# Attention in a hybrid decoder block: score and value products as three fp32r products of parts

## Chip, cores, metric

The kernel runs on 1 core of one Trainium2 chip. The time is the device time of one execution in microseconds; a run's figure is that of its slowest core, here its only one. Engines are named as in the profile: PE is TensorE's matmul, PEld its weight load, DVE is VectorE, ACT is ScalarE, POOL is GpSimd, SP is SyncE.

## What is computed

One layer over 256 tokens of width 2048, all in float32. The part that the change touches is the attention branch: 16 heads of 128, causal, softmax with a linear bias. With one block of 256 tokens only the own block counts, so per head it is:

```python
q = rms_norm(q, q_norm_w);  k = rms_norm(k, k_norm_w)          # (256, 128) each
s = q @ k.T * 128 ** -0.5 - slope * (t_q - t_k)                 # masked where t_q < t_k
p = softmax(s)                                                  # (256, 256), lower triangle
attn = p @ v                                                    # (256, 128)
```

Around it stand the input projection (x @ w_in, 2048 x 18496), a Mamba-2 SSD branch, the output projections, gates, and an MLP of width 8192. Those weight products make nearly all of the work.

## The kernel before

**The weight stream.** All large products run as a stream of blocks. A block is 2048 rows by 512 columns of a weight matrix, taken in 8 units of 256 rows. SP loads a unit into one of four `raw` slots; ACT rounds it to fp32r (`whi`, L941); DVE subtracts to get the rest (`wlo`, L1463); PE runs 12 products of 512 columns per unit (L645 to L647: x_hi whi, x_hi wlo, x_lo whi). ACT and DVE work three units ahead of PE (`LEAD = 3`). On each engine the other work is put into this stream by hand: `steps(b, {step: [functions]})` on ACT and DVE runs the functions of a step behind the split of the unit three ahead; `stream(..., after={s: [...]})` on PE runs them behind unit s. Each engine runs its instructions in the order written.

**Attention.** The 16 heads go in four groups of four. Group g's q, k and v come out of the blocks 3g, 3g+1 and 3g+2. ACT copies them out of PSUM (L1009 to L1019), they are normed, turned by DMA transposes of their 16-bit halves and joined by DVE in `qk_both` (`q_join` L1575, `k_join` L1586). ACT copies `qk_both` with the norm weight to `qT` (L1037) and `kT` (L1053). The heads of group g run within the next three blocks (24 steps), five steps apart: scores on PE behind step 5h+1, bias and maximum on DVE, exp on ACT, the norm on DVE, the halves on ACT, a DMA transpose from SP's queue, `p_join` on DVE at step 5h+6 (L1631, L1633, out to `probT`), weights times values on PE behind step 5h+7, and the split of the result into `aT_hi` and `aT_lo` (L1077, L1639).

Causality leaves 3 of 4 tiles. So a head has one score product of 256 columns (queries of the second half against all keys, L718) and one of 128 (first half, L719), and in the same way one value product of 256 columns (L695) and one of 128 (L696). All four are plain fp32. PE shows a plain fp32 product as two records, an fp32r product as one.

**Other small products** of the kernel stay as they are: the dt projection in fp32r with 256 columns (L737 to L741), the SSD products in fp32 with 64 columns (L818), three fp32r products of 512 columns (L806), fp32 ones of 256 and 128 columns (L829, L830), and transposes of 128 columns (L597).

Of the kernel before, what the change touches and what calls it, by code (L numbers as in the profile page):

```python
# [23 lines left out]
T = 256  # L24
P = 128
NTOK = T // P
HD = 128
# [16 lines left out]
COLS = 512  # L44
# [8 lines left out]
B_QKV = 0  # L53
# [8 lines left out]
def build(nc, x, mix_norm_w, w_in, q_norm_w, k_norm_w, conv_w, conv_b, dt_bias, a_log, d_skip, ssm_norm_w,  # L62
          w_attn_out, w_ssm_out, w_out, mlp_norm_w, w_up, w_down, out):
    f32 = mybir.dt.float32
    f32r = mybir.dt.float32r
# [10 lines left out]
    with ctx:  # L76
# [6 lines left out]
        def sb(name, region, off, shape, dt=f32):  # L83
            return nc.alloc_sbuf_tensor_at(name, shape, dt, offset=BASE + at[region] + off)
# [16 lines left out]

        q_st = sb("q_st", "C", 0, [P, NTOK, COLS])
        k_st = sb("k_st", "C", 4 * KB, [P, NTOK, COLS])
        v_st = sb("v_st", "C", 8 * KB, [P, NTOK, COLS])
        sq = sb("sq", "C", 12 * KB, [P, 8, HD])
        qT = sb("qT", "C", 16 * KB, [P, 4, T])
        kT = sb("kT", "C", 20 * KB, [P, 4, T])
        qk_half = sb("qk_half", "E", 0, [P, 2, NTOK, COLS], u16)
        q_tiles = sb("q_tiles", "E", 4 * KB, [P, 2, NTOK * 4, P], u16)
        k_tiles = sb("k_tiles", "E", 12 * KB, [P, 2, NTOK * 4, P], u16)  # L110
        qk_both = sb("qk_both", "E", 8 * KB, [P, 4, T])
        prob = sb("prob", "C", 24 * KB, [P, 3 * P])
        probT = sb("probT", "C", 24 * KB + 1536, [P, 3 * P])
        dist = sb("dist", "C", 24 * KB + 3072, [P, 3 * P])
        dist_i = sb("dist_i", "C", 24 * KB + 4608, [P, 3 * P], i32)
        p_half = sb("p_half", "C", 24 * KB + 4608, [P, 2, 3 * P], u16)
# [112 lines left out]
        def sem(name):  # L229
            return ctx.enter_context(nc.semaphore(name))  # L230
# [64 lines left out]
        p_halved = sem("p_halved")  # L295
        p_turned = sem("p_turned")
        probT_ready = sem("probT_ready")
        pv = sem("pv")
        aT_hi_done = sem("aT_hi_done")
        aT_lo_done = sem("aT_lo_done")  # L300
# [74 lines left out]
        def fp(ap):  # L375

            return ap.bitcast(f32)

        def halves(ap):
            return ap.bitcast(u16).rearrange("p (n a) -> p a n", a=2)  # L380
# [212 lines left out]
        def _(pe):  # L593
# [94 lines left out]
            def at_pv(n, hh, g):  # L688
                def f():
                    pe.wait_ge(probT_ready, n + 1)  # L690
                    if hh == 0:
                        pe.wait_ge(set_free[2], g + 1)
                    if later(n):
                        pe.wait_ge(aT_lo_done, n)
                    mm(ps[7][:, 0:T], v_st[:, 0, hh * HD:(hh + 1) * HD], probT[:, 0:T], start=True, stop=False)  # L695
                    mm(ps[7][:, P:T], v_st[:, 1, hh * HD:(hh + 1) * HD], probT[:, T:T + P], start=False,  # L696
                       stop=True).then_inc(pv, 1)
                return f

            def attention(g):  # L700

                n0 = 4 * g
                a = [{} for _ in range(3)]

                def put(step, f):
                    a[step // 8].setdefault(step % 8, []).append(f)
                put(1, lambda: pe.wait_ge(kT_ready, g + 1))
                put(1, lambda: pe.wait_ge(qT_ready, g + 1))
                for hh in range(4):
                    put(5 * hh + 1, at_scores(n0 + hh, hh))  # L710
                    put(5 * hh + 7, at_pv(n0 + hh, hh, g))
                return a

            def at_scores(n, hh):
                def f():
                    if later(n):
                        pe.wait_ge(biased, n)
                    mm(ps[6][:, 0:T], qT[:, hh, P:T], kT[:, hh, :], start=True, stop=True)  # L718
                    mm(ps[6][:, T:T + P], qT[:, hh, 0:P], kT[:, hh, 0:P], start=True, stop=True).then_inc(scores, 1)  # L719
                return f  # L720

            def par_transposes():
# [208 lines left out]
        def _(act):  # L931
# [81 lines left out]
            def evac_v(g):  # L1013
                def f():
                    block_done(B_QKV + 3 * g + 2)
                    if later(g):
                        act.wait_ge(pv, 4 * g)
                    A(v_st[:, 0, :], SETS[2][0][:, :], ACT.Copy, scale=rstd1[:, 0:1])
                    A(v_st[:, 1, :], SETS[2][1][:, :], ACT.Copy, scale=rstd1[:, 1:2]).then_inc(set_free[2], 1)  # L1019
                return f  # L1020

            def q_halve(g):
# [8 lines left out]
            def copy_qT(g):  # L1031
                def f():
                    act.wait_ge(q_joined, g + 1)
                    act.wait_ge(const_ready, 2)
                    if later(g):
                        act.wait_ge(scores, 4 * g)
                    A(qT[:, :, :], qk_both[:, :, :], ACT.Copy, scale=par[:, QN_C:QN_C + 1]).then_inc(qT_ready, 1)  # L1037
                return f

            def k_halve(g):  # L1040
# [7 lines left out]
            def copy_kT(g):  # L1048
                def f():
                    act.wait_ge(k_joined, g + 1)  # L1050
                    if later(g):
                        act.wait_ge(scores, 4 * g)
                    A(kT[:, :, :], qk_both[:, :, :], ACT.Copy, scale=par[:, KN_C:KN_C + 1]).then_inc(kT_ready, 1)  # L1053
                return f

            def at_exp(n):
# [9 lines left out]
            def p_halve(n):  # L1066
                def f():
                    act.wait_ge(normed, 2 * n + 2)
                    if later(n):
                        act.wait_ge(p_turned, 16 * n)  # L1070
                    A(p_half[:, :, :], halves(prob[:, :]), ACT.Copy).then_inc(p_halved, 1)
                return f

            def at_hi(n):
                def f():
                    act.wait_ge(pv, n + 1)
                    A(aT_hi[:, bass.ds(n, 1), :].rearrange("p a t -> p (a t)"), ps[7][:, 0:T], ACT.Copy) \  # L1077
                        .then_inc(aT_hi_done, 1)
                return f

            def attention(n0):
                a = [{} for _ in range(3)]

                def put(step, f):
                    a[step // 8].setdefault(step % 8, []).append(f)
                for hh in range(4):
                    put(5 * hh + 3, p_halve(n0 + hh))
                for hh in range(4):
                    put(5 * hh + 2, at_exp(n0 + hh))
                    put(5 * hh + 8, at_hi(n0 + hh))  # L1090
                return a
# [363 lines left out]
        def _(dve):  # L1455
# [119 lines left out]
            def q_join(g):  # L1575
# [7 lines left out]
                    i.then_inc(q_joined, 1)  # L1583
                return f

            def k_join(g):  # L1586
                def f():
                    dve.wait_ge(k_turned, 32 * g + 32)
                    dve.wait_ge(qT_ready, g + 1)
                    for a in range(2):  # L1590
                        i = V.tensor_copy(halves(qk_both[:, :, :].rearrange("p c t -> p (c t)"))[:, a, :],
                                          k_tiles[:, a, :, :].rearrange("p (t c) l -> p c t l", t=NTOK))
                    i.then_inc(k_joined, 1)
                return f
# [31 lines left out]
            def p_join(n):  # L1626
                def f():
                    dve.wait_ge(p_turned, 16 * n + 16)
                    if later(n):
                        dve.wait_ge(pv, n)  # L1630
                    V.tensor_copy(halves(probT[:, :])[:, :, P:3 * P],  # L1631
                                  p_tiles[:, :, 0:2, :].rearrange("p a c l -> p a (c l)"))
                    V.tensor_copy(halves(probT[:, :])[:, :, 0:P], p_tiles[:, :, 2, :]).then_inc(probT_ready, 1)  # L1633
                return f

            def at_lo(n):
# [7 lines left out]
            def attention(n0, g):  # L1644
                a = [{} for _ in range(3)]
                slope_group[0] = g

                def put(step, f):
                    a[step // 8].setdefault(step % 8, []).append(f)
                for hh in range(4):  # L1650
                    put(5 * hh + 6, p_join(n0 + hh))
                for hh in range(4):
                    put(5 * hh + 1, at_bias(n0 + hh, hh))
                    put(5 * hh + 2, at_norm(n0 + hh))
                    put(5 * hh + 8, at_lo(n0 + hh))
                return a

            def add(d, step, f):
                d.setdefault(step, []).append(f)
                return d  # L1660

            steps(B_QKV, {5: [dtw_rest], 6: [x_mean]}, early={s: [x_lo(XLEAD + s)] for s in range(US - XLEAD)})
            steps(B_QKV + 1, {2: [dt_chain], 4: [qk_sums(0, 0)], 5: [qk_norm(0, 0, q_st)]})
            steps(B_QKV + 2, {1: [qk_sums(0, 1)], 2: [dec_chain], 3: [qk_norm(0, 1, k_st), q_join(0)], 7: [k_join(0)]})
            def qkv_group(g):
                a = attention(4 * g - 4, g - 1)
                add(a[1], 1, qk_sums(g, 0))
                add(a[1], 3, qk_norm(g, 0, q_st))
                add(a[2], 1, qk_sums(g, 1))
                add(a[2], 3, qk_norm(g, 1, k_st))  # L1670
                add(a[2], 4, q_join(g))
                add(a[2], 7, k_join(g))
                for i in range(3):
                    steps(B_QKV + 3 * g + i, a[i])
# [543 lines left out]
```

## Time and profile before

| | |
|---|---|
| median of 3 runs | 2001.96 us (2001.77 to 2002.26) |
| the profiled execution | 2002.14 us |
| its span, first to last instruction | 2000.4 us |
| TensorE clock granted, mean | 1.000 |
| PE busy | 1995.2 us (100%), 9010 records |
| PEld busy | 1658.9 us (83%) |
| DVE busy | 1276.0 us (64%) |
| ACT busy | 1111.4 us (56%) |
| POOL busy | 192.1 us (10%) |
| DMA | 418.99 MB, mean 209 GB/s |

The span lies 1.7 us under the time of its own execution. Ends of PE records are modelled and records overlap (a product of 512 columns shows 389 ns and the next starts 0.23 us after it), so what a product costs is read from the distance of starts, or from the chain of waits, which lists pieces without overlap.

### The profile page before, as it was taken

Reading aid. Unit: us, or ns where it says so; the run is one execution under the profiler, and the core shown is the slowest. Engines: PE = TensorE matmul, PEld = TensorE weight load, DVE = VectorE, ACT = ScalarE, POOL = GpSimd, SP = SyncE. Lnnn points to the kernel's source line nnn. Section 1 sums busy time; section 2 is a strip of 40 time slices with the busy share of each in tenths; the row PEclk is TensorE's granted clock in tenths of the full one; section 3 lists DMA queues with packets and bytes.
Section 4 is the critical chain, followed back from the end, with each engine's and each line's share of the span. In section 5 each row is a group of like instructions: output and inputs, shape, how many; then the busy total and the mean of one; then the engine's idle time right before and its main releaser. Section 6 shows DMA issues by size and latency. Waiting matters only on the chain.

```text
span 2000.4 us, 25399 instructions
## 1 busy us (share of the span) xinstructions
PE 1995.2 (100%) x9010; PEld 1658.9 (83%) x9010; DVE 1276.0 (64%) x1477; ACT 1111.4 (56%) x1257; POOL 192.1 (10%) x190
## 2 busy tenths in 40 slices
PE   9999999999999999999999999999999999999999
PEld 8888888888888888888888888888888888888887
DVE  5676676777787666666675565656545555654554
ACT  6565666667776454545764444555445445544542
POOL 2110120112222111110000000010000000000000
PEclk9999999999999999999999999999999999999999
DMA  7777887789996666566896667767667766766775
GB/s 247 212 199 198 215 203 202 213 229 243 244 240 212 198 194 196 189 189 189 231 237 204 200 207 237 207 191 222 207 192 205 225 192 193 224 205 186 216 220 163
DMA packets 330895, 418.99 MB, mean 209 GB/s; under 512 B 145184, under 2 KB 146400, under 8 KB 330544
## 3 DMA queue, kind: packets, MB, share of 16 engines
q1 hardware_dynamic: 329104, 414.19, 71.8%
q10 hardware_dynamic: 1232, 2.75, 0.4%
q8 instruction: 60, 0.98, 0.2%
q0 software_dynamic: 464, 0.77, 0.2%
q14 instruction: 35, 0.29, 0.0%
HBM read 382.46 MB, written 2.16 MB: 192 GB/s over the span
## 4 chain that ended last, share of the span: by engine, by line
PE 99%; DMA 0%; DVE 0%; SPq 0%; ACT 0%; issue 0%; DVEq 0%
PE ps L645 32%; PE ps L647 32%; PE ps L646 32%; PE ps L818 1%; DMA raw<-in_w_in 0%; PE ps L718 0%; PE ps L695 0%; PE ps L806 0%; PE ps L597 0%; PE ps L696 0%; PE ps L719 0%; PE ps L829 0%; PE ps L739 0%; PE ps L741 0%; PE ps L830 0%; DVE wlo L1463 0%
## 5 line engine op out<-in xcount | busy, mean ns | idle before, releaser
L1463 DVE TENSOR_TENSOR wlo<-raw,whi 128x1024 fp32r<-128x1024 f32 x703 | 882.6, 1262 | 631.5 <-ACT whi L941 629.9
L941 ACT ACTIVATE whi<-raw 128x1024 fp32r<-128x1024 f32 x703 | 739.7, 1058 | 681.7 <-PE ps L647 665.0
L645 PE MATMUL ps<-whi,xT_hi 128*128 128x512 f32 x1272 | 500.4, 393 | 0.6 <-DVE xT_lo L1487 0.6
L647 PE MATMUL ps<-whi,xT_lo 128*128 128x512 f32 x1272 | 495.8, 390 | 0.0
L646 PE MATMUL ps<-wlo,xT_hi 128*128 128x512 f32 x1272 | 495.1, 389 | 0.0
L647 PEld LDWEIGHTS ps<-whi,xT_lo 128*128 128x128 f32 x1272 | 238.8, 188 | 50.3
L645 PEld LDWEIGHTS ps<-whi,xT_hi 128*128 128x128 f32 x1272 | 239.0, 188 | 48.6 <-DVE xT_lo L1487 0.9
L646 PEld LDWEIGHTS ps<-wlo,xT_hi 128*128 128x128 f32 x1272 | 239.2, 188 | 48.0
L645 PE MATMUL ps<-whi,hT_hi 128*128 128x512 f32 x512 | 199.4, 389 | 0.0
L647 PE MATMUL ps<-whi,fT_lo 128*128 128x512 f32 x512 | 199.3, 389 | 0.0
L646 PE MATMUL ps<-wlo,fT_hi 128*128 128x512 f32 x512 | 199.3, 389 | 0.0
L647 PE MATMUL ps<-whi,hT_lo 128*128 128x512 f32 x512 | 199.3, 389 | 0.0
L646 PE MATMUL ps<-wlo,hT_hi 128*128 128x512 f32 x512 | 199.3, 389 | 0.0
L645 PE MATMUL ps<-whi,fT_hi 128*128 128x512 f32 x512 | 199.3, 389 | 0.0
L647 PEld LDWEIGHTS ps<-whi,hT_lo 128*128 128x128 f32 x512 | 96.1, 188 | 20.0
L647 PEld LDWEIGHTS ps<-whi,fT_lo 128*128 128x128 f32 x512 | 96.1, 188 | 19.9
L645 PEld LDWEIGHTS ps<-whi,fT_hi 128*128 128x128 f32 x512 | 96.1, 188 | 19.9
L646 PEld LDWEIGHTS ps<-wlo,fT_hi 128*128 128x128 f32 x512 | 96.1, 188 | 19.9
L645 PEld LDWEIGHTS ps<-whi,hT_hi 128*128 128x128 f32 x512 | 96.1, 188 | 19.9
L646 PEld LDWEIGHTS ps<-wlo,hT_hi 128*128 128x128 f32 x512 | 96.1, 188 | 19.8
L646 PE MATMUL ps<-wlo,sT_hi 128*128 128x512 f32 x256 | 99.7, 389 | 0.0
L645 PE MATMUL ps<-whi,sT_hi 128*128 128x512 f32 x256 | 99.6, 389 | 0.0
(271 smaller groups left out, 1930.4 us busy)
## 6 DMA issues: line engine op xcount, KB each, us to landing
raw<-in_w_in SPq DMA_DIRECT2D x319, 512.0 KB, 4.3
raw<-in_w_up SPq DMA_DIRECT2D x128, 512.0 KB, 4.0
raw<-in_w_down SPq DMA_DIRECT2D x128, 512.0 KB, 4.3
raw<-in_w_ssm_out SPq DMA_DIRECT2D x64, 512.0 KB, 4.1
raw<-in_w_attn_out SPq DMA_DIRECT2D x32, 512.0 KB, 4.4
raw<-in_w_out SPq DMA_DIRECT2D x32, 512.0 KB, 4.1
arow<-arows SPq DMA_DIRECT2D x16, 512.0 KB, 4.9
h<-in_x ACTq DMA_DIRECT2D x1, 2048.0 KB, 10.4
```

Source lines behind the costliest of these rows:

```text
L645: mm(dst, xh, whi[sl][:, kk, :], start=(s == 0 and kk == 0), stop=False)
L646: mm(dst, xh, wlo[sl][:, kk, :], start=False, stop=False)
L647: last = mm(dst, xl, whi[sl][:, kk, :], start=False, stop=(s == US - 1 and kk == UK - 1))
L818: last = mm(ps[6][:, hh * SHD:(hh + 1) * SHD], M[:, hh, :], xf[:, hh, :], start=True, stop=True)
L941: A(whi[s % SLOTS][:, :, :], raw[s % SLOTS][:, :, :], ACT.Copy).then_inc(hi_ready, 1)
L1463: V.tensor_tensor(wlo[s % SLOTS][:, :, :], raw[s % SLOTS][:, :, :], fp(whi[s % SLOTS][:, :, :]), ALU.subtract).then_inc(lo_ready, 1)
```

## The change

Each of q, k, v and the softmax weights is kept as two fp32r tiles: the value rounded (hi) and the rest (lo). Each of the four products of a head becomes three: hi hi, lo hi, hi lo. ACT's copies write the hi tiles in place of the fp32 ones; DVE computes q, k and v rests once per group (`q_rest`, `k_rest`, `v_rest`) and, per head, the rest of the softmax weights behind a new rounding on ACT (`p_round`). The scores now run the 128-column product first, the value products keep the 256-column one first. PE waits for the rests; PSUM set 2 is given back by DVE in `v_rest`, no longer by ACT. The lo tiles lie in other, free memory. The diff:

```diff
-        v_st = sb("v_st", "C", 8 * KB, [P, NTOK, COLS])
+        v_hi = sb("v_hi", "C", 8 * KB, [P, NTOK, COLS], f32r)
+        v_lo = sb("v_lo", "W", 8 * KB, [P, NTOK, COLS], f32r)
...
@@ at_pv (PE)
-                    mm(ps[7][:, 0:T], v_st[:, 0, hh * HD:(hh + 1) * HD], probT[:, 0:T], start=True, stop=False)
-                    mm(ps[7][:, P:T], v_st[:, 1, hh * HD:(hh + 1) * HD], probT[:, T:T + P], start=False,
-                       stop=True).then_inc(pv, 1)
+                    hd = slice(hh * HD, (hh + 1) * HD)
+                    for i, (v, p) in enumerate(((v_hi, p_hi), (v_lo, p_hi), (v_hi, p_lo))):
+                        mm(ps[7][:, 0:T], v[:, 0, hd], p[:, 0:T], start=(i == 0), stop=False)
+                    for i, (v, p) in enumerate(((v_hi, p_hi), (v_lo, p_hi), (v_hi, p_lo))):
+                        last = mm(ps[7][:, P:T], v[:, 1, hd], p[:, T:T + P], start=False, stop=(i == 2))
+                    last.then_inc(pv, 1)
@@ attention (PE)
                 put(1, lambda: pe.wait_ge(kT_ready, g + 1))
-                put(1, lambda: pe.wait_ge(qT_ready, g + 1))
+                put(1, lambda: pe.wait_ge(q_split, g + 1))
+                put(1, lambda: pe.wait_ge(k_split, g + 1))
@@ at_scores (PE)
-                    mm(ps[6][:, 0:T], qT[:, hh, P:T], kT[:, hh, :], start=True, stop=True)
-                    mm(ps[6][:, T:T + P], qT[:, hh, 0:P], kT[:, hh, 0:P], start=True, stop=True).then_inc(scores, 1)
+                    for i, (q, k) in enumerate(((qT_hi, kT_hi), (qT_lo, kT_hi), (qT_hi, kT_lo))):
+                        mm(ps[6][:, T:T + P], q[:, hh, 0:P], k[:, hh, 0:P], start=(i == 0), stop=(i == 2))
+                    for i, (q, k) in enumerate(((qT_hi, kT_hi), (qT_lo, kT_hi), (qT_hi, kT_lo))):
+                        last = mm(ps[6][:, 0:T], q[:, hh, P:T], k[:, hh, :], start=(i == 0), stop=(i == 2))
+                    last.then_inc(scores, 1)
@@ evac_v (ACT)
-                    A(v_st[:, 1, :], SETS[2][1][:, :], ACT.Copy, scale=rstd1[:, 1:2]).then_inc(set_free[2], 1)
+                    A(v_hi[:, 1, :], SETS[2][1][:, :], ACT.Copy, scale=rstd1[:, 1:2]).then_inc(v_rounded, 1)
@@ (ACT) new; attention: put(5 * hh + 6, p_round(n0 + hh))
+            def p_round(n):
+                def f():
+                    act.wait_ge(p_joined, n + 1)
+                    A(p_hi[:, :], probT[:, :], ACT.Copy).then_inc(p_rounded, 1)
@@ (DVE) new; attention: put(0, k_rest(g)), put(3, v_rest(g)); q_rest at step 6 of the v block
+            def q_rest(g):
+                def f():
+                    dve.wait_ge(qT_ready, g + 1)
+                    V.scalar_tensor_tensor(qT_lo[:, :, :], qk_both[:, :, :], par[:, QN_C:QN_C + 1], fp(qT_hi[:, :, :]),
+                                           ALU.mult, ALU.subtract).then_inc(q_split, 1)
...
+            def v_rest(g):
+                def f():
+                    dve.wait_ge(v_rounded, g + 1)
+                    dve.wait_ge(rstd1_ready, 1)
+                    V.scalar_tensor_tensor(v_lo[:, 0, :], SETS[2][0][:, :], rstd1[:, 0:1], fp(v_hi[:, 0, :]), ALU.mult,
+                                           ALU.subtract)
+                    V.scalar_tensor_tensor(v_lo[:, 1, :], SETS[2][1][:, :], rstd1[:, 1:2], fp(v_hi[:, 1, :]), ALU.mult,
+                                           ALU.subtract).then_inc(set_free[2], 1)
@@ k_join (DVE)
-                    dve.wait_ge(qT_ready, g + 1)
+                    dve.wait_ge(q_split, g + 1)
@@ p_join (DVE)
-                    V.tensor_copy(halves(probT[:, :])[:, :, 0:P], p_tiles[:, :, 2, :]).then_inc(probT_ready, 1)
+                    V.tensor_copy(halves(probT[:, :])[:, :, 0:P], p_tiles[:, :, 2, :]).then_inc(p_joined, 1)
+                    dve.wait_ge(p_rounded, n + 1)
+                    V.tensor_tensor(p_lo[:, :], probT[:, :], fp(p_hi[:, :]), ALU.subtract).then_inc(probT_ready, 1)
```

`k_rest` is as `q_rest`, with `kT_ready`, `kT_hi`, `kT_lo`, the key's norm weight and `k_split`; `copy_qT` and `copy_kT` write `qT_hi` and `kT_hi`.

## Rows read from the trace of the kernel before

**Rows 1.** Page, engines and chain that ended last: busy us, shares of the span
```profile
PE 1995.2 (100%) x9010; PEld 1658.9 (83%) x9010; DVE 1276.0 (64%) x1477; ACT 1111.4 (56%) x1257; POOL 192.1 (10%) x190
...
PE 99%; DMA 0%; DVE 0%; SPq 0%; ACT 0%; issue 0%; DVEq 0%
```

**Rows 2.** Waits, whole span: who waited for whom, us in total, times, longest
```profile
ACT whi L941 <- PE ps L647: 665.0, 450, 4.8
```

**Rows 3.** Chain around the first head's scores: start us, us until the next piece
```profile
88.39 0.43 PE ps L718 x2
88.82 0.22 PE ps L719 x2
89.04 0.23 PE ps L645
```

**Rows 4.** Attention's records on PE: duration ns min/median/max, first and last start
```profile
L718 PE MATMUL ps<-kT,qT x32: 377/377/378, 88.2 to 344.8; 128*128 128x256 f32 x32
...
L696 PE MATMUL ps<-probT,v_st x32: 272/274/276, 106.3 to 362.8; 128*128 128x128 f32 x32
```

**Rows 5.** Chain, 36 to 40.5 us: fp32r products of 256 columns (dt)
```profile
36.59 1.81 PE ps L739 x16
38.41 1.80 PE ps L741 x15
```

**Rows 6.** Chain, 575.3 to 578.5 us: fp32 products of 64 columns, and the next
```profile
575.95 1.73 PE ps L818 x16
577.68 0.29 PE ps L645
```

**Rows 7.** Chain, 1218 to 1221 us: transposes of 128 columns, one record each
```profile
1219.34 0.87 PE ps L597 x8
```

**Rows 8.** Timeline of the weight loads (PEld) after one head's scores: start us, us
```profile
188.41 0.40 PEld L719 LDWEIGHTS ps<-kT,qT 128*128 128x128 f32 x2
188.73 0.19 PEld L645 LDWEIGHTS ps<-whi,xT_hi 128*128 128x128 f32 x1
188.84 0.19 PEld L646 LDWEIGHTS ps<-wlo,xT_hi 128*128 128x128 f32 x1
```

**Rows 9.** Timelines, ACT and PE: transposed keys against the scores of their group
```profile
85.67 1.15 ACT L1053 ACTIVATE kT<-qk_both,par 128x1024 f32<-128x1024 f32 x1 [0.47 <-DVE qk_both L1591]
...
88.00 0.39 PE L647 MATMUL ps<-whi,xT_lo 128*128 128x512 f32 x1
88.23 0.59 PE L718 MATMUL ps<-kT,qT 128*128 128x256 f32 x2
...
L1053 ACT ACTIVATE kT<-qk_both,par x4: 1147/1150/1154, 85.7 to 297.2; 128x1024 f32<-128x1024 f32 x4
...
300.39 0.59 PE L718 MATMUL ps<-kT,qT 128*128 128x256 f32 x2
```

**Rows 10.** DVE and ACT groups by form (count, busy us, mean ns, idle before)
```profile
L1603 DVE SCALAR_TENSOR_TENSOR prob<-dist,negslope,ps 128x384 f32<-128x384 f32 x16 | 9.8, 611 | 5.5 <-PE ps L719 5.4
L1795 DVE SCALAR_TENSOR_TENSOR zs<-ps,rstd,zs 128x512 f32<-128x512 f32 x16 | 11.3, 744 | 11.9 <-ACT zs L1238 11.9
...
L1788 DVE TENSOR_TENSOR xd_lo<-xd,xd_hi 128x512 fp32r<-128x512 f32 x8 | 5.4, 681 | 0.0
...
L1639 DVE TENSOR_TENSOR aT_lo<-ps,aT_hi 128x256 f32 x8 | 3.3, 418 | 0.5 <-ACT aT_hi L1077 0.5
...
L1228 ACT ACTIVATE xd_hi<-xd 128x512 fp32r<-128x512 f32 x8 | 4.9, 614 | 0.0
```

**Rows 11.** Timelines, DVE and PE: last head's transposed weights against their use
```profile
359.66 0.30 DVE L1633 COPY probT<-p_tiles 128x256 uint16<-128x256 uint16 x1
...
362.04 0.39 PE L647 MATMUL ps<-whi,xT_lo 128*128 128x512 f32 x1
362.27 0.59 PE L695 MATMUL ps<-probT,v_st 128*128 128x256 f32 x2
```

**Rows 12.** 85 to 370 us: busy PE, PEld, DVE, ACT, POOL (count); clock; DMA
```profile
85.00:370.00 285.00, 285.00 (x1291) 237.30 (x1291) 198.54 (x299) 176.65 (x244) 32.48 (x22) 1.00 0.79 205
```

More of the change, by code:

```diff
@@ L103, in build @@
         k_st = sb("k_st", "C", 4 * KB, [P, NTOK, COLS])
-        v_st = sb("v_st", "C", 8 * KB, [P, NTOK, COLS])
+        v_hi = sb("v_hi", "C", 8 * KB, [P, NTOK, COLS], f32r)
+        v_lo = sb("v_lo", "W", 8 * KB, [P, NTOK, COLS], f32r)
         sq = sb("sq", "C", 12 * KB, [P, 8, HD])
-        qT = sb("qT", "C", 16 * KB, [P, 4, T])
-        kT = sb("kT", "C", 20 * KB, [P, 4, T])
+        qT_hi = sb("qT_hi", "C", 16 * KB, [P, 4, T], f32r)
+        qT_lo = sb("qT_lo", "W", 14 * KB, [P, 4, T], f32r)
+        kT_hi = sb("kT_hi", "C", 20 * KB, [P, 4, T], f32r)
+        kT_lo = sb("kT_lo", "W", 4 * KB, [P, 4, T], f32r)
         qk_half = sb("qk_half", "E", 0, [P, 2, NTOK, COLS], u16)
@@ L113, in build @@
         probT = sb("probT", "C", 24 * KB + 1536, [P, 3 * P])
+        p_hi = sb("p_hi", "W", 18 * KB, [P, 3 * P], f32r)
+        p_lo = sb("p_lo", "W", 18 * KB + 1536, [P, 3 * P], f32r)
         dist = sb("dist", "C", 24 * KB + 3072, [P, 3 * P])
@@ L297, in build @@
         probT_ready = sem("probT_ready")
+        p_joined = sem("p_joined")
+        p_rounded = sem("p_rounded")
+        q_split = sem("q_split")
+        k_split = sem("k_split")
+        v_rounded = sem("v_rounded")
         pv = sem("pv")
@@ L1017, in f @@
                         act.wait_ge(pv, 4 * g)
-                    A(v_st[:, 0, :], SETS[2][0][:, :], ACT.Copy, scale=rstd1[:, 0:1])
-                    A(v_st[:, 1, :], SETS[2][1][:, :], ACT.Copy, scale=rstd1[:, 1:2]).then_inc(set_free[2], 1)
+                    A(v_hi[:, 0, :], SETS[2][0][:, :], ACT.Copy, scale=rstd1[:, 0:1])
+                    A(v_hi[:, 1, :], SETS[2][1][:, :], ACT.Copy, scale=rstd1[:, 1:2]).then_inc(v_rounded, 1)
                 return f
@@ L1036, in f @@
                         act.wait_ge(scores, 4 * g)
-                    A(qT[:, :, :], qk_both[:, :, :], ACT.Copy, scale=par[:, QN_C:QN_C + 1]).then_inc(qT_ready, 1)
+                    A(qT_hi[:, :, :], qk_both[:, :, :], ACT.Copy, scale=par[:, QN_C:QN_C + 1]).then_inc(qT_ready, 1)
                 return f
@@ L1052, in f @@
                         act.wait_ge(scores, 4 * g)
-                    A(kT[:, :, :], qk_both[:, :, :], ACT.Copy, scale=par[:, KN_C:KN_C + 1]).then_inc(kT_ready, 1)
+                    A(kT_hi[:, :, :], qk_both[:, :, :], ACT.Copy, scale=par[:, KN_C:KN_C + 1]).then_inc(kT_ready, 1)
                 return f
@@ L1072, in p_halve @@
                 return f
+            def p_round(n):
+                def f():
+                    act.wait_ge(p_joined, n + 1)
+                    A(p_hi[:, :], probT[:, :], ACT.Copy).then_inc(p_rounded, 1)
+                return f
             def at_hi(n):
@@ L1087, in attention @@
                     put(5 * hh + 3, p_halve(n0 + hh))
+                    put(5 * hh + 6, p_round(n0 + hh))
                 for hh in range(4):
@@ L1584, in q_join, with k_rest, f @@
                 return f
+            def q_rest(g):
[3 more added lines that the diff above has]
+                                           ALU.mult, ALU.subtract).then_inc(q_split, 1)
+                return f
+            def k_rest(g):
+                def f():
+                    dve.wait_ge(kT_ready, g + 1)
+                    V.scalar_tensor_tensor(kT_lo[:, :, :], qk_both[:, :, :], par[:, KN_C:KN_C + 1], fp(kT_hi[:, :, :]),
+                                           ALU.mult, ALU.subtract).then_inc(k_split, 1)
+                return f
+            def v_rest(g):
+                def f():
+                    dve.wait_ge(v_rounded, g + 1)
[4 more added lines that the diff above has]
+                                           ALU.subtract).then_inc(set_free[2], 1)
+                return f
             def k_join(g):
@@ L1649, in put @@
                     a[step // 8].setdefault(step % 8, []).append(f)
+                put(0, k_rest(g))
+                put(3, v_rest(g))
                 for hh in range(4):
@@ L1663, in _ @@
             steps(B_QKV + 1, {2: [dt_chain], 4: [qk_sums(0, 0)], 5: [qk_norm(0, 0, q_st)]})
-            steps(B_QKV + 2, {1: [qk_sums(0, 1)], 2: [dec_chain], 3: [qk_norm(0, 1, k_st), q_join(0)], 7: [k_join(0)]})
+            steps(B_QKV + 2, {1: [qk_sums(0, 1)], 2: [dec_chain], 3: [qk_norm(0, 1, k_st), q_join(0)], 6: [q_rest(0)], 7: [k_join(0)]})
             def qkv_group(g):
@@ L1671, in qkv_group @@
                 add(a[2], 4, q_join(g))
+                add(a[2], 6, q_rest(g))
                 add(a[2], 7, k_join(g))
```

## The prediction

> **What bounds the kernel now.** I read the page first. PE is busy for the whole span, and the chain that ended last is PE for 99% of it [rows 1]. The waits agree: the longest one is ACT waiting for PE to free a weight slot, 665 us in all [rows 2]. So the time is the sum of what PE's products take, one behind another, and two things can move it: the PE time of the changed products, and a wait that lets PE stand. About 0.2% (4 us) is what a measurement of this kernel can tell from no change.
>
> The durations of PE records overlap and don't add up. What adds up is the chain, whose pieces run from one start to the next. It gives a head's scores 0.43 us for the 256-column product (two fp32 records) and 0.22 us for the 128-column one (two records), 0.65 us together, and a product of 512 columns in fp32r 0.23 us [rows 3]. The value products have the same records: 377 and 274 ns long, 32 of each, which is two per head for 16 heads [rows 4]. So attention's products hold PE for 16 x 2 x 0.65 = 20.8 us of 2000.4: the change can't do much either way.
>
> **What one fp32r product costs.** For 256 columns the trace has it: 16 in 1.81 us and 15 in 1.80 us, 0.113 us with 64 columns of weights and 0.120 us with 128, as here [rows 5]. Three cost 0.36 us where the fp32 product cost 0.43.
>
> For 128 columns in fp32r the trace has no row. Near rows show a floor. An fp32 record of 64 columns takes 1.73 / 16 = 0.108 us [rows 6], as much as one of 128 columns (0.22 / 2), so with so few columns the time isn't set by them. A transpose of 128 columns in one record takes 0.87 / 8 = 0.109 us [rows 7]. The loads of weights show why: the load for L645, which is fp32r, starts 0.11 us ahead of the next one, for L646, while short products run [rows 8]. Each product brings its own load, and I read 0.11 us as what one load holds up the next. The bounds: 0.23 / 4 = 0.057 us if only the columns counted, and 0.22 us if it were carried out like the fp32 product. Between them I take 0.109 us, the row nearest in form (one record, four-byte data, 128 columns, 128 columns of weights); if it is paced as the 256-column one it is 0.120 us.
>
> The Trainium skill (TensorE: Matmul & The Clock Gate, Back-to-back issue gap) gives about 81 ns for a product of 128 columns that brings its load. By that three would cost 0.24 us, a head's pair 0.60 us, and the change would win 1.5 us. The same page (LDWEIGHTS) works a load out as its columns over 1.2 GHz, 107 ns for 128; by that rule, the trace agrees with 0.11 us [rows 8], and that goes against the 81 ns.
>
> **The change, part by part.**
> - *Products on PE.* Each head's pair goes from 0.65 us to 3 x 0.109 + 3 x 0.120 = 0.687 us, +0.037 us. There are 32 pairs (scores and values, 16 heads): +1.2 us, all on the path. At 0.120 us for the short ones it is 0.72 us, and 0.06 us more where short products stand ahead of the stream (the product behind the 64-column ones took 0.29 us, not 0.23 [rows 6]), so 0.78 us at most: +4.2 us. The order (short ones first in the scores, last in the values) changes nothing in the sum.
> - *Rest of q, once a group.* DVE, 128x1024. The same operation takes 611 ns for 384 elements and 744 ns for 512 [rows 10], 1.04 ns each, so 1.28 us. It stands at step 6 of the v block, three steps of 2.7 us ahead of the group's first scores, and they cover it.
> - *Rest of k, once a group.* Also 1.28 us, but it stands straight before the scores. In the first group ACT's copy of k ends at 85.67 + 1.15 = 86.82 us; the rest ends at 88.10, and PE hears of it near 88.15. The scores started at 88.23, but their weight load starts with the product before, at 88.00 [rows 9]. That load comes 0.15 us late: up to 0.2 us. In the last group the copy ends near 298.4, the rest at 299.7, and the scores started at 300.39 [rows 9]: nothing. I take +0.2 us in all, with 0 and 0.8 us (four groups) as ends.
> - *Rest of v, once a group.* Two operations of 512 elements, 0.74 us each [rows 10], at step 3, with the first use behind step 7: four steps of 12 x 0.23 = 2.7 us as cover. The PSUM set goes back some 11 us later than now; its next use is a block (22 us) after that. Nothing.
> - *Softmax weights, each head.* ACT's rounding of 384 elements lies between 0.37 and 0.61 us (256 elements and 512 [rows 10]; I take 0.55); DVE's rest between 0.42 and 0.68 us [rows 10], 0.55 taken; with two hand-overs of 0.05 us it is 1.2 us, at most 1.4. The last head has its weights at 359.96 us, and PE's load for them starts near 362.04 [rows 11]: 2.1 us of cover, 0.7 to 0.9 us left over.
> - *Behind those waits.* DVE stands in `p_join` for ACT's rounding. Behind it are the next head's bias and maximum, then its exp, norm and halves, and SP's transpose, which holds SP's next weight loads. ACT in turn stands for DVE's join ahead of its next split. Each is about 1.2 us later at worst, while both work three units of 2.7 us ahead of PE. Nothing reaches PE; if the lead were gone, each late unit would cost what it is late.
> - *Load of the engines.* DVE gets 4 x (2 x 1.28 + 2 x 0.74) + 16 x 0.55 = 25 us more in the 285 us of the heads, on 198.5 busy; ACT 16 x 0.55 = 9 us on 176.7 [rows 12]. Neither becomes the bound. Copies that write fp32r instead of fp32 have the same size. No DMA is added.
>
> **Sum**: 1.2 + 0.2 = +1.4 us. The profiled execution took 2002.14 us with a span of 2000.4, so 1.7 us lie outside it; that gives 2003.5 us for it. The median of the runs is 0.2 us lower: 2003.4 us.
>
> **Rivals.**
> 1. *Short fp32r products are carried out as fp32 ones.* Nothing in the trace has fp32r below 256 columns, so nothing excludes it. Then a 128-column product costs 0.22 us in two records, and three of them 0.66; a pair is 1.02 us, +0.37 us, times 32 = +11.8 us; with the wait +12.0, 2014.0 us. It decides from 0.16 us on: there the change passes 4 us. For it: plain fp32 takes two slow records for the same numbers, and the fast form is shown for wide ones alone. Against: the fp32r load is no slower than the others [rows 8], and the load explains every short row without a second rule. 30%. This ends on the slower side.
> 2. *Only columns count.* A short product costs 0.057 us, a pair 3 x 0.057 + 0.36 = 0.53 us, -0.12 us, times 32 = -3.8 us: 1998.2 us, and 1.5 us lower if the wide ones take 0.113 us without a load to wait for. Against it stand the 64-column records, as dear as 128-column ones [rows 6]. 7%.
> 3. *PE waits in each head.* If the chain of the softmax weights took 3 us instead of 1.2, PE would stand 0.9 us in each of 16 heads: +14 us, 2018 us. It decides from 2.1 us on. For it: two engines wait for each other in the middle of their splits. Against: the sizes above. 5%.
>
> **How the numbers follow.** My forecast, the load as the floor, has 58%: 2003.4 us, its own range 2002 to 2006.5. Rival 1 has 30%, so the range must take it in, to 2015 us; the low end, 2001, takes in a forecast whose short products come a little below 0.109. Left out are nearly all of rivals 2 and 3. Faster by over 0.2%: 0.03, the far end of rival 2. Slower: 0.30 + 0.05 + 0.02 (the far end of my own) = 0.37. Within 0.2%: 0.60.
>
> **What would show it.** In the chain after, a head's scores should be a piece of three short products of about 0.33 us and one of three wide ones of about 0.36 us; PE should have 192 fp32r records for attention (six per pair) where it had 128, with short ones 0.11 us apart. Starts 0.22 us apart, or six records for three products, show rival 1. A gap ahead of the first scores of a group is the rest of k; a wait of PE for `p_lo` is rival 3. I am wrong altogether if the weight units come late in the attention part, which would show as PE waiting for `wlo`.

## The result, and the profile after

The changed kernel takes 2006.43 us, median of 16 runs (2005.69 to 2007.24); the kernel before, on the same chips, 2002.04 us (2001.70 to 2002.97). The ratio is 1.0021 with a 95% interval of 1.0014 to 1.0027: 4.4 us slower. The forecast was 2003.4 us with a range of 2001 to 2015.

The page of the kernel after, span, engines and chain (they answer to [rows 1]):

```profile
span 2004.7 us, 25588 instructions
...
PE 1999.0 (100%) x9074; PEld 1660.7 (83%) x9074; DVE 1299.0 (65%) x1509; ACT 1117.1 (56%) x1273; POOL 191.4 (10%) x190
...
PE 94%; issue 2%; DMA 1%; DVE 1%; ACT 1%; POOL 0%; SPq 0%; ACTq 0%; DVEq 0%; POOLq 0%
```

The span grew by 4.3 us, from 2000.4 us. PE has 64 records more, DVE 23 us more of work, ACT 6 us. The chain is where the two pages differ most: it was PE for 99% and is PE for 94% now. The walk back from the end no longer stays on PE. It leaves it at the first scores of group 3 (232.4 us, back to 172.3) and of group 1 (88.8 us, back to 43.2) for DVE and then for the preparation of q and k, so at these two moments PE was not what set the time. The missing 5% are the length of these two stretches, in which PE is busy too; they are no measure of how long it waited, which is 0.44 and 0.35 us.

The chain around the first head's value products (start, us until the next piece), against [rows 3]:

```profile
106.56 0.23 PE ps L657
106.79 0.35 PE ps L707 x3
107.14 0.29 PE ps L709 x3
107.43 0.28 PE ps L655
107.71 0.23 PE ps L656
```

Three wide products (L707) and three short ones (L709) stand where two records each stood. The wide ones take 0.35 us, the short ones 0.29, and the product of the stream behind them 0.28 us instead of 0.23. The boundaries between pieces lie a little differently in the two kernels, so a pair is better measured between products of the stream: from the first product of the pair to the second one behind it, less the 0.227 us of a product of 512 columns. By that measure each of the 32 pairs before took 0.656 us, and after 24 of the 32 took 0.692 to 0.693 us, the other 8 some 0.08 to 0.11 us more.

The eight that cost more are the ones that PE waited for. The timeline of PE at the first of them, the scores of head 0 (start, us, engine, line, and the wait where the profile shows one):

```profile
88.24 0.39 PE L657 MATMUL ps<-whi,xT_lo 128*128 128x512 f32 x1
88.82 0.30 PE L733 MATMUL ps<-kT_hi,qT_hi 128*128 128x128 f32 x1 [0.19 <-DVE kT_lo L1620]
88.95 0.28 PE L733 MATMUL ps<-kT_hi,qT_lo 128*128 128x128 f32 x1
89.07 0.27 PE L733 MATMUL ps<-kT_lo,qT_hi 128*128 128x128 f32 x1
89.18 0.33 PE L735 MATMUL ps<-kT_hi,qT_hi 128*128 128x256 f32 x1
...
89.58 0.40 PE L655 MATMUL ps<-whi,xT_hi 128*128 128x512 f32 x1
```

The product before starts at 88.24 and would be followed 0.23 us later. The first score product starts at 88.82, 0.35 us late. The products behind it start 0.11 to 0.13 us apart, and all six are through when the stream goes on at 89.58, 0.76 us later. The weight loads of the same stretch:

```profile
88.02 0.19 PEld L657 LDWEIGHTS ps<-whi,xT_lo 128*128 128x128 f32 x1
88.79 0.19 PEld L733 LDWEIGHTS ps<-kT_hi,qT_hi 128*128 128x128 f32 x1 [0.58 <-issue]
88.90 0.19 PEld L733 LDWEIGHTS ps<-kT_hi,qT_lo 128*128 128x128 f32 x1
89.00 0.19 PEld L733 LDWEIGHTS ps<-kT_lo,qT_hi 128*128 128x128 f32 x1
```

The same load for the second head's scores, which waited for nothing:

```profile
102.97 0.19 PEld L733 LDWEIGHTS ps<-kT_hi,qT_hi 128*128 128x128 f32 x1
```

The second head's load starts at 102.97, with the product before it, and its own product follows at 103.19. The first head's load would have started in the same way at 88.24. It starts at 88.79, and its product at 88.82 as the profile models it. The second product of the pair then comes 0.13 us behind the first, where without a wait it comes 0.06 us behind (103.25), and the pair takes 0.77 us, 0.08 more than 0.692. I read this as a load that behind a wait has no product to hide under.

The same count over all 32 pairs gives the account of the profiled execution:

| term | us |
|---|---|
| 32 pairs, 0.692 in place of 0.656 us | +1.17 |
| the stream between the pairs, some stretches 0.02 us longer | +0.15 |
| waits of PE ahead of the four groups' first scores: 0.35, 0.22, 0.44, 0.35 | +1.36 |
| waits ahead of value products: third heads of the first three groups 0.14, 0.13, 0.14, a fourth head 0.06 | +0.47 |
| weight loads that the eight waits lay open, 0.08 to 0.11 each | +0.78 |
| the start, up to 88 us, ahead of any attention (it varies by 0.7 us over these profiles) | +0.24 |
| behind the last pair | +0.16 |
| sum, of 4.3 | +4.33 |

So products are about a third of it, 1.3 us. Some 2.6 us are PE's waits for the rests and the loads behind these waits.

**The wait for k.** Group 3's turn, DVE, then ACT, then PE (timelines):

```profile
225.50 1.28 DVE L1613 SCALAR_TENSOR_TENSOR qT_lo<-qk_both,par,qT_hi 128x1024 fp32r<-128x1024 f32 x1
226.70 1.22 DVE L1487 TENSOR_TENSOR wlo<-raw,whi 128x1024 fp32r<-128x1024 f32 x1
227.83 0.42 DVE L1689 TENSOR_TENSOR aT_lo<-ps,aT_hi 128x256 f32 x1
228.17 1.38 DVE L1639 COPY qk_both<-k_tiles 128x1024 uint16<-128x1024 uint16 x2
229.43 1.22 DVE L1487 TENSOR_TENSOR wlo<-raw,whi 128x1024 fp32r<-128x1024 f32 x1
230.86 1.28 DVE L1620 SCALAR_TENSOR_TENSOR kT_lo<-qk_both,par,kT_hi 128x1024 fp32r<-128x1024 f32 x1 [0.21 <-ACT kT_hi L1070]
```

```profile
229.67 1.16 ACT L1070 ACTIVATE kT_hi<-qk_both,par 128x1024 fp32r<-128x1024 f32 x1 [0.74 <-DVE qk_both L1639]
```

```profile
231.73 0.39 PE L657 MATMUL ps<-whi,xT_lo 128*128 128x512 f32 x1
232.39 0.32 PE L733 MATMUL ps<-kT_hi,qT_hi 128*128 128x128 f32 x1 [0.28 <-DVE kT_lo L1620]
```

Read upwards from the scores at 232.39, which start 0.44 us late: the rest of k (1.28 us) ends at 232.14; it waited for DVE's split (229.43) and for ACT's copy (229.67 to 230.83); the copy waited for the join of k (228.17 to 229.55); and the join stood behind the rest of q (225.50), a split and the low part of a head's result. The rest of k was predicted there. That the rest of q stands in the same queue ahead of the join was not.

**The wait for the softmax weights** of the third head of the first group, DVE, then ACT:

```profile
133.02 2.07 DVE L1487 TENSOR_TENSOR wlo<-raw,whi 128x1024 fp32r<-128x1024 f32 x1 [2.59 <-ACT whi L958]
135.01 0.45 DVE L1679 COPY probT<-p_tiles 128x512 uint16<-128x512 uint16 x1
135.36 0.29 DVE L1681 COPY probT<-p_tiles 128x256 uint16<-128x256 uint16 x1
136.24 0.56 DVE L1683 TENSOR_TENSOR p_lo<-probT,p_hi 128x384 fp32r<-128x384 f32 x1 [0.59 <-ACT p_hi L1094]
```

```profile
131.92 1.06 ACT L958 ACTIVATE whi<-raw 128x1024 fp32r<-128x1024 f32 x1
135.68 0.53 ACT L1094 ACTIVATE p_hi<-probT 128x384 fp32r<-128x384 f32 x1 [2.70 <-DVE probT L1681]
```

DVE waited 2.6 us for ACT's rounding of a weight unit, since ACT was behind copying k out of PSUM (up to 132.0). Its split then took 2.07 us instead of 1.23, so the join ended at 135.65. The way over ACT and back added 1.15 us, to 136.80, and the value product started at 136.86, 0.14 us late. In the kernel before, the same split took 2.07 us too. DVE, then PE, before:

```profile
134.49 0.29 DVE L1633 COPY probT<-p_tiles 128x256 uint16<-128x256 uint16 x1
```

```profile
135.60 0.39 PE L647 MATMUL ps<-whi,xT_lo 128*128 128x512 f32 x1
135.83 0.38 PE L695 MATMUL ps<-probT,v_st 128*128 128x256 f32 x1
```

The join ended at 134.78, and the value product's weight load starts with the product before it, at 135.60. So this head had 0.8 us of cover, not 2.1.

### The profile page after: what moved, and what is told of

It is laid out like the page before. It is cut to its first block, busy times and chain, and to the rows that moved or that the text cites. A ratio compares the mean times of both kernels' runs of the same rounds, so it can differ in the third digit from the quotient of the medians.

```text
span 2004.7 us, 25588 instructions
## 1 busy us (share of the span) xinstructions
PE 1999.0 (100%) x9074; PEld 1660.7 (83%) x9074; DVE 1299.0 (65%) x1509; ACT 1117.1 (56%) x1273; POOL 191.4 (10%) x190
## 4 chain that ended last, share of the span: by engine, by line
PE 94%; issue 2%; DMA 1%; DVE 1%; ACT 1%; POOL 0%; SPq 0%; ACTq 0%; DVEq 0%; POOLq 0%
PE ps L655 30%; PE ps L657 30%; PE ps L656 30%; PE ps L835 1%; POOL rqk L2161 0%; DMA x_in<-in_x 0%; DMA q_tiles<-qk_half 0%; PE ps L607 0%; PE ps L823 0%; DMA k_tiles<-qk_half 0%; ACT whi L958 0%; PE ps L735 0%; PE ps L707 0%; PE ps L733 0%; DVE wlo L1487 0%
## 6 DMA issues: line engine op xcount, KB each, us to landing
h<-in_x ACTq DMA_DIRECT2D x1, 2048.0 KB, 10.4
```

## Experiments

Each ran beside the kernel before, whose medians were then 2002.07 to 2002.21 us. "Waits" are those of PE ahead of attention products in the profiled execution.

**e1: the products alone.** All rests and their waits are taken out, and each product is three fp32r products of the hi parts (in the value products the values themselves stand in for the softmax weights). So the result leaves out the low parts and is not attention.

```diff
-                    for i, (q, k) in enumerate(((qT_hi, kT_hi), (qT_lo, kT_hi), (qT_hi, kT_lo))):
+                    for i, (q, k) in enumerate(((qT_hi, kT_hi), (qT_hi, kT_hi), (qT_hi, kT_hi))):
...
-                put(0, k_rest(g))
-                put(3, v_rest(g))
```

> Leaves out the four rests: each product is three fp32r products of the hi parts (the value products take values in place of the softmax weights), and the waits are those of the kernel before. Theory A (the trace of after: a pair costs about 0.045 us more, 32 pairs, and 1.8 us are waits for the rests): +1.4 us on the kernel before, 2003.4 us, no gap ahead of any attention product. Rival B (the products cost more than the distances of starts show, and the waits are small): +4 us, 2006 us.

2003.59 us (11 runs, 2003.17 to 2003.80) against 2002.14: +1.45 us. No waits; 32 pairs of 0.692 to 0.693 us. The same pieces of the chain as above:

```profile
106.25 0.35 PE ps L707 x3
106.61 0.29 PE ps L709 x3
106.89 0.28 PE ps L655
```

They are as long as in the changed kernel. The pairs give 32 x 0.037 = 1.2 us; from the first pair to the last, with the stream between them, e1 is 1.37 us longer than the kernel before. So the products cost 1.2 to 1.45 us. Rival B, that they make all of the difference, is out.

**e2: the rests alone.** The other half: all rests and waits, but each product one plain fp32 product (of the hi parts).

```diff
-                    for i, (q, k) in enumerate(((qT_hi, kT_hi), (qT_lo, kT_hi), (qT_hi, kT_lo))):
-                        mm(ps[6][:, T:T + P], q[:, hh, 0:P], k[:, hh, 0:P], start=(i == 0), stop=(i == 2))
...
+                    mm(ps[6][:, T:T + P], fp(qT_hi[:, hh, 0:P]), fp(kT_hi[:, hh, 0:P]), start=True, stop=True)
+                    mm(ps[6][:, 0:T], fp(qT_hi[:, hh, P:T]), fp(kT_hi[:, hh, :]), start=True, stop=True).then_inc(scores, 1)
```

> All rests and their waits as in the changed kernel, but each product is one plain fp32 product of the hi parts as before (the low parts are left out of the result). Theory A: the waits alone, about 0.35 us ahead of each group's first scores and 0.13 us ahead of the third head's value product, +1.5 to +2 us: 2003.8 us. Rival B: +0.3 us or less, 2002.3 us.

2005.81 us (2005.08 to 2006.12) against 2002.14: +3.7 us, where I expected at most 2. The profiled execution has waits of 2.88 us (one of 1.20 us ahead of the second group's first scores) and pairs that are 0.83 us longer in all, the exposed loads: 3.7 us, which is the difference. The rests cost PE time with no product changed. My number was too low for two reasons: I had left out the exposed loads, and one wait, the second group's, is not the same from kernel to kernel. It was 0.22 us in the changed kernel.

**e3: no rest of q.** Products take the hi part of q in its place.

```diff
-                add(a[2], 6, q_rest(g))
...
-                    dve.wait_ge(q_split, g + 1)
+                    dve.wait_ge(qT_ready, g + 1)
```

> The changed kernel without the rest of q (its products take the hi part in its place). Theory A, in its part that the rest of q stands ahead of the join of k on DVE and delays it: the gap ahead of the first scores falls below 0.1 us in groups 2 to 4 and stays near 0.35 us in the first, where the DMA transposes set the join; 0.7 to 1.0 us less than the changed kernel, 2005.6 us. Rival C (the rest of k alone makes the gap): all four gaps stay, 2006.4 us.

2004.75 us, 1.7 us under the changed kernel, and the 11 runs fall into two clusters: six at 2004.26 to 2004.75 and five at 2005.64 to 2006.47. The waits ahead of the first scores are 0.13 and 1.05 us in the first two groups and none in the last two, as expected of theory A (in group 3 a load of 0.09 us is still exposed). The first group's wait fell too, which I had not expected; it varies by itself, since in e10, which changes nothing ahead of it, it is 0.25 us. And the second group's grew to 1.05 us, in a profiled execution of 2005.75 us, one of the upper five. DVE and PE there:

```profile
156.30 1.39 DVE L1639 COPY qk_both<-k_tiles 128x1024 uint16<-128x1024 uint16 x2 [1.97 <-DMA k_tiles<-qk_half]
...
159.00 1.28 DVE L1620 SCALAR_TENSOR_TENSOR kT_lo<-qk_both,par,kT_hi 128x1024 fp32r<-128x1024 f32 x1 [0.21 <-ACT kT_hi L1070]
```

```profile
160.53 0.43 PE L733 MATMUL ps<-kT_hi,qT_hi 128*128 128x128 f32 x2 [0.89 <-DVE kT_lo L1620]
```

Now the join itself waits, 1.97 us, and for a DMA: the transpose of k that SP issued at 149.03.

```profile
149.03 1.97 SPq L426 DMA_TRANSPOSE k_tiles<-qk_half  x1
```

From issue to landing this transpose took 7.2 us here, 6.9 in the kernel before, 7.1 and 7.3 in e4 and e2, and 5.6 in the changed kernel. In the kernel before, the join had slack for it; with the rest of k behind it there is none, and PE passes on what the transfer varies by. So the changed kernel's 0.22 us in this group belongs to an early landing. In e10 the transpose took 7.1 us too, but it was issued 1.3 us earlier than in the changed kernel, and 0.14 us of wait was left. That the two clusters of runs come from this landing is my reading of the profiles; it isn't shown run by run.

**e4: the rest of q one step earlier.** The same work as the changed kernel.

```diff
-                add(a[2], 6, q_rest(g))
+                add(a[2], 5, q_rest(g))
```

> The changed kernel with the rest of q one step earlier on DVE (step 5, behind the last head's join of softmax weights, in place of step 6), the same work. Theory A: DVE has idle time there, so the join of k comes up to 1.2 us earlier and the gaps of groups 2 to 4 fall below 0.15 us: 2005.7 us. Rival C: no change, 2006.4 us.

2005.02 us (2004.37 to 2006.91), 1.4 us under the changed kernel, again in two clusters (six up to 2005.02, five from 2005.69). Waits ahead of first scores 0.17, 0.90, 0 and 0; the ones ahead of value products as in the changed kernel (0.48 us in all). A change of place does what leaving the rest out does: in groups 3 and 4 the wait needs the rest of q ahead of the join. It is not the only thing that the wait needs, as e9 and e10 show.

**e5: waits moved away, all work kept.** The rest of q as in e4; k rounded and its rest taken in two pieces, head 0 first; the third head's join and rounding ahead of the splits of their step.

```diff
-                    A(kT_hi[:, :, :], qk_both[:, :, :], ACT.Copy, scale=par[:, KN_C:KN_C + 1]).then_inc(kT_ready, 1)
+                    A(kT_hi[:, 0, :], qk_both[:, 0, :], ACT.Copy, scale=par[:, KN_C:KN_C + 1]).then_inc(kT_ready, 1)
+                    A(kT_hi[:, 1:4, :], qk_both[:, 1:4, :], ACT.Copy, scale=par[:, KN_C:KN_C + 1]).then_inc(kT_ready, 1)
...
-                    steps(B_QKV + 3 * g + i, a[i])
+                    steps(B_QKV + 3 * g + i, a[i], early=early[i])
```

Here `early` holds the rest of head 0's k for the first block and the third head's join for the third.

> The changed kernel, all work kept, with three moves: the rest of q at step 5; k rounded and its rest taken in two pieces, head 0 first (the rest of head 0 ahead of DVE's split at step 0); the third head's join and rounding of softmax weights ahead of the splits of its step, where both engines stood idle. Theory A (the surplus over the product price is waits): all gaps ahead of attention products go, and it takes the time of the products-only kernel, 2003.5 us. Rival B (waits are only shifted to later ones, or DVE's load holds the stream back): 2005 us or more.

2004.44 us (2004.10 to 2005.05) against 2002.07. In the attention part it is just what was expected: no wait, 32 pairs of 0.69 us, the last value product 1.18 us later than in the kernel before. But the time is 0.9 us over the 2003.5 expected, and in the profiled execution that lies elsewhere, in the MLP, whose code is the same. The wait there (us in total, times, longest), and DVE at that place:

```profile
PE ps L655 <- DVE fT_lo L2063: 0.8, 1, 0.8
```

```profile
1402.52 1.39 DVE L2055 COPY f_st<-f_half 128x1024 uint16<-128x1024 uint16 x2 [2.71 <-DMA f_half<-r_half]
```

DVE waited 2.7 us for a transpose of MLP activations and PE's first product on them started 0.9 us late. In this profile the slowest of these transposes landed after 6.8 us, in that of the kernel before after 6.0. The other profiles agree: e5 to e9 each have one such wait, of 0.28 to 0.92 us, and a slowest landing of 6.3 to 6.8 us; the other seven have none, and 4.8 to 6.0 us. So the surplus in this profile is a wait of the same kind in a place that I had not touched, and the expectation missed by it. All 11 runs of e5 lie at 2004.1 us or above; whether each has this wait isn't shown, nor why the transposes land late in some kernels.

**e6: six short products in place of three**, otherwise as e1.

```diff
-                    for i, (q, k) in enumerate(((qT_hi, kT_hi), (qT_hi, kT_hi), (qT_hi, kT_hi))):
+                    for i, (q, k) in enumerate(((qT_hi, kT_hi),) * 6):
```

> Products only, as in the first experiment, with six fp32r products of 128 columns in place of three in each pair (the result leaves out the low parts and counts the short products six times). Theory A (a weight load of 0.107 us is what a short product costs): 32 x 3 x 0.107 = +10.3 us on the products-only kernel, 2013.9 us. Rival D (a short product costs its columns, 0.057 us, and the pair's 0.69 us has another cause): +5.5 us, 2009.1 us.

2014.03 us (5 runs, 2013.81 to 2014.19) against 2003.59 for e1: +10.4 us for 96 more products, 0.109 us each. Rival D, at +5.5 us, falls. The chain:

```profile
106.46 0.35 PE ps L707 x3
106.81 0.62 PE ps L709 x6
107.44 0.29 PE ps L655
```

Six take 0.62 us where three took 0.29: 0.11 us for each one more. A pair went from 0.692 to 1.03 us, +0.34. The last digit is not firm: from the first pair to the last the profiles differ by 9.96 us, 0.104 us a product, and this one has a wait of 0.43 us in the MLP.

**e9 and e10: the moves of e5 one at a time.** e9 takes only the two pieces of k, e10 only the third head's join and rounding:

```diff
+                    steps(B_QKV + 3 * g + i, a[i], early={0: [k_rest(g - 1, 0)]} if i == 0 else None)
```

```diff
+                    steps(B_QKV + 3 * g + i, a[i], early={0: [p_join(4 * g - 2)]} if i == 2 else None)
```

> The changed kernel with k rounded and its rest taken in two pieces, head 0 first and ahead of DVE's split; nothing else moved. Theory A: the path from the join of k to the first scores falls from 2.7 to about 1.1 us, so the gaps ahead of the groups' first scores (1.35 us in the profile of the changed kernel, and 0.1 us of exposed weight load behind each) go, and those of the third and fourth head's value products (0.48 us and 0.1 each) stay: 2004.6 us. Rival C (DVE is late as a whole): gaps of 0.2 us or more stay ahead of the first scores, 2006 us.

> The changed kernel with only the third head's join and rounding of the softmax weights moved ahead of the splits of their step. Theory A: the gaps ahead of the third (and fourth) head's value product go, 0.48 us and four exposed loads of 0.1 us, those ahead of first scores stay or shrink: 2005.5 us. Rival C (moved work makes the splits late): PE waits for wlo, 2006.5 us or more.

e9: 2005.13 us (2004.60 to 2005.45); the waits ahead of first scores are gone, three of 0.13 to 0.14 us ahead of third heads' value products are left, and PE waits once in the MLP, 0.68 us, as in e5; that accounts for the 0.5 us over what I expected. e10: 2004.25 us (2003.89 to 2004.67), much better than I expected. It took away the waits for the softmax weights, and of those for k it left 0.25 and 0.14 us in the first two groups and none in the last two. DVE at group 3's turn, and PE at its scores:

```profile
226.30 1.40 DVE L1641 COPY qk_both<-k_tiles 128x1024 uint16<-128x1024 uint16 x2
227.96 1.22 DVE L1489 TENSOR_TENSOR wlo<-raw,whi 128x1024 fp32r<-128x1024 f32 x1 [0.26 <-ACT whi L958]
229.10 1.28 DVE L1622 SCALAR_TENSOR_TENSOR kT_lo<-qk_both,par,kT_hi 128x1024 fp32r<-128x1024 f32 x1
```

```profile
230.72 0.39 PE L657 MATMUL ps<-whi,xT_lo 128*128 128x512 f32 x1
230.95 0.22 PE L733 MATMUL ps<-kT_hi,qT_hi 128*128 128x128 f32 x1
```

The join of k starts at 226.30 where it started at 228.17 in the changed kernel, 1.9 us earlier, while PE itself was only 1.0 us earlier there (the product ahead of the scores starts at 230.72 and at 231.73). The rest of q still stands in its old place. So the third head's join, some 20 us before, had been pushing the preparation of k back. The two kernels' DVE timelines show how. The next head's bias (L1651, in e10 L1653) starts at 208.34 in the changed kernel and at 206.48 in e10, the split at 219.99 and 218.12, the rest of q at 225.50 and 223.63, the join of k at 228.17 and 226.30: 1.9 us apart each time. Where DVE stands still longest in between, it is for ACT's rounding of a unit (0.84 and 1.43 us in the changed kernel), and ACT had stood just before for DVE's norm of k and for its join of the fourth head's weights (1.07 and 1.86 us). The two engines hand the delay to each other, and none of their idle time takes it up.

So in groups 3 and 4 three different moves end the same wait: the rest of q one step earlier (e4), k in pieces (e9), and the third head's join ahead of the splits (e10). The wait is what several delays on one path come to beyond its cover, and none of them is its only cause.

**e8 and e7: the wide products only.** Since a short fp32 product costs 0.22 us and three short fp32r ones 0.33, the short ones were left in plain fp32. e8 is this without rests, as e1; e7 is the whole computation, with fp32 copies of the halves of q, k and v that the short products read, with rests for the wide products only, and with the moves of e5.

```diff
-                    for i, (q, k) in enumerate(((qT_hi, kT_hi), (qT_lo, kT_hi), (qT_hi, kT_lo))):
-                        mm(ps[6][:, T:T + P], q[:, hh, 0:P], k[:, hh, 0:P], start=(i == 0), stop=(i == 2))
+                    mm(ps[6][:, T:T + P], q_f[:, hh, :], k_f[:, hh, :], start=True, stop=True)
...
-                    A(qT_hi[:, :, :], qk_both[:, :, :], ACT.Copy, scale=par[:, QN_C:QN_C + 1]).then_inc(qT_ready, 1)
+                    A(q_f[:, :, :], qk_both[:, :, 0:P], ACT.Copy, scale=par[:, QN_C:QN_C + 1])
+                    A(qT_hi[:, :, P:T], qk_both[:, :, P:T], ACT.Copy, scale=par[:, QN_C:QN_C + 1]).then_inc(qT_ready, 1)
```

> Products only, no rests (hi parts, and values in place of the softmax weights, so the result leaves the rest out): the 256-column products as three fp32r products, the 128-column ones as one fp32 product. Theory A: 32 x (0.58 - 0.653) = -2.3 us on the kernel before, 1999.8 us, and no gap. If the three wide products cost more beside fp32 ones: 2001 us or more.

> Only the products of 256 columns as three fp32r products; those of 128 columns stay one fp32 product, from fp32 copies of their half of q, k and v. Moves as in e5; the rests of q, v and the softmax weights cover only what the wide products read. Nothing is left out. Theory A: a pair takes 3 x 0.12 + 0.22 = 0.58 us where it took 0.653, 32 pairs, -2.3 us on the kernel before, 1999.8 us, if no wait is left. Rival B (waits come back): 2001 us or more.

e8: 2000.12 us (1999.79 to 2000.41). e7: 2000.09 us (11 runs, 1999.58 to 2000.41) against 2002.07 us (27 runs, 2001.56 to 2002.53); the ratio is 0.9990, 95% interval 0.9981 to 0.9999. Both are 2.0 us under the kernel before, 0.3 us short of the 2.3 expected. e7 is the fastest kernel here that computes everything, and 6.3 us under the changed one. No wait ahead of any attention product, and a pair takes 0.583 us. Page and chain of e7:

```profile
span 1998.2 us, 25548 instructions
...
PE 1992.8 (100%) x9042; PEld 1657.3 (83%) x9042; DVE 1294.8 (65%) x1509; ACT 1119.1 (56%) x1285; POOL 190.1 (10%) x190
```

```profile
105.39 0.35 PE ps L710 x3
105.74 0.22 PE ps L711 x2
105.96 0.23 PE ps L658
```

0.35 us for three wide products, 0.22 for the fp32 one in two records, and the stream goes on at 0.23. The 32 pairs give 2.3 us; a wait in the MLP takes 0.56 us in this profile.

## Why the prediction was right, and where it was not

The range held the time (2006.4 in 2001 to 2015). The likeliest value was 3 us too low. It was given 0.60 that no change could be told; the time moved by 0.2%, just over that bound.

In part the range held by luck. It reached to 2015 for rival 1, which did not happen. My own forecast reached to 2006.5 for short products at 0.120 us, 4.2 us in all, and these cost 1.2 to 1.45. What filled the gap were waits that I had taken for 0.2 us.

- *Products on PE* was right. Predicted 0.687 us a pair and +1.2 us, measured 0.692 and +1.2 by the pairs, +1.45 as a time (e1). The step rested on short products being paced by their weight load, taken as 0.109 us: e6 measured 0.104 to 0.113, and 0.109 by its run time. By the rule for a load, the columns over 1.2 GHz (the Trainium skill, TensorE: Matmul & The Clock Gate, LDWEIGHTS), 107 ns were due, and e6's trace agrees; the 81 ns of its section on back-to-back issue don't hold for fp32r here.
- *Rival 1*, short fp32r products carried out as fp32 ones, is out: a short product shows one record, and a pair is 0.692 us, not 1.02. *Rival 2* is out by e6. Two side sums of theirs were wrong: by its own terms rival 1 passes 4 us from 0.14 us a short product on, not 0.16, and wide products at 0.113 us would have given rival 2 0.7 us more, not 1.5.
- *Rest of k, once a group* is the step that failed most. I took 0.2 us in all with 0.8 as the far end; the waits are 1.36 us, and the exposed loads behind them 0.36 us more. I had measured its cover in the kernel before, as if nothing ahead of it would move. In the last group, where I saw 0.7 us to spare, PE waited 0.35.
- *Rest of q* was costed at nothing because the first scores lie three steps behind it. True for its reader, but not for its queue: the join of k stands behind it on DVE, and with the rest one step earlier (e4) the waits of groups 3 and 4 were gone.
- *Softmax weights*: the size was right (1.15 us against 1.2), the cover was read at one head only. I took the 2.1 us of the last head for all; the third heads of the first three groups had 0.8, the others 1.7 to 2.8.
- *Behind those waits* named the next head's chain and said that nothing reaches PE. e10 shows that it does: DVE and ACT carried 1.9 us of delay on to the preparation of k at the end of the same block.
- *An exposed weight load* behind each wait, 0.1 us, was in no term. For waits of 0.13 us it nearly doubles them.
- *Load of the engines* held: DVE is busy for 215.3 of the 285 us, 17 us more than the 198.5 before [rows 12] where I had counted 25. Its load as a whole was not the bound; the order of its queue was what PE waited for.

Mechanism and size of the product term were right; the waits were mis-sized, 0.2 us against 2.6 with their loads.

## What to carry to other kernels

Three fp32r products replace one fp32 product with a gain only where the columns outlast the weight load: here 0.36 us for 0.43 at 256 columns, but 0.33 for 0.22 at 128. Other widths were not tried. And work that is added to a queue is not covered by the time to its own reader alone: go through everything that stands behind it in that queue, and read the cover at each instance, not at one.

## What the runs showed that I had not expected

- A wait of PE in a dense stream costs its length and some 0.1 us more, since the next weight load has no product to hide under (eight pairs of 0.77 to 0.80 us beside 24 of 0.692).
- A DMA transpose lands 3.1 to 8.0 us after its issue in these twelve profiles, and the same one differs from kernel to kernel: k's second in group 2 took 5.6 us in the changed kernel and 7.1 to 7.3 in e2 to e4. Where its join had little cover, PE waited for the difference (group 2 in e2 to e4, the MLP in e5 to e9).
- A delay of 1.9 us on DVE behind one head's join was still there in full 20 us later, in another step's work (e10).
